# Attention with transposed scores: row scores issued two units ahead, in two PSUM banks instead of three, transposed scores two blocks ahead in three

## The reference

```python
def sink_attention(qg, k, v, sink, valid):       # 8 heads of 64, 2 key heads
    s = jnp.einsum('bqhgd,bkhd->bhgqk', qg, k).astype(jnp.float32) * ATTN_SCALE
    if valid is not None:
        s = jnp.where(valid, s, NEG_INF)         # window of +-128 tokens, and 256 context tokens
    ...
    p = jax.nn.softmax(jnp.concatenate([s, sink_col], axis=-1), axis=-1)[..., :-1]
    return jnp.einsum('bhgqk,bkhd->bqhgd', p, v.astype(jnp.float32))
```

## Time and profile before

| what | us |
|---|---|
| median of 3 runs (lowest, highest) | 3675.62 (3671.17, 3679.07) |
| profiled execution, device time | 3673.01 |
| its span, first to last instruction | 3671.2 |
| TensorE busy in the span | 2980.1 (81%) |
| VectorE busy | 1621.3 (44%) |
| ScalarE busy | 1228.6 (33%) |
| mean granted TensorE clock | 0.896 |

### The profile page before, as it was taken

How to read it: one execution, slowest core, us unless ns; L and a number is a source line. 1 busy time by engine, 2 the same in 40 slices (tenths; PEclk the granted TensorE clock), 3 DMA queues, 4 the chain that set the end, 5 groups by cost and what they waited for, 6 DMA issues and landing times. The chain is left out here.

```text
span 3671.2 us, 36461 instructions
## 1 busy us (share of the span) xinstructions
PE 2980.1 (81%) x14078; PEld 2311.5 (63%) x14078; DVE 1621.3 (44%) x2617; ACT 1228.6 (33%) x1972; POOL 160.5 (4%) x258
## 2 busy tenths in 40 slices
PE   7799997857775979996894799999788288848893
PEld 2577874536664848884663689888555166737773
DVE  1566334537774130005552335421233453347786
ACT  2444212434553041113422321111233211227786
POOL 0000000100000000000000000000000010020002
PEclk9899998988997979996887999999899588869997
DMA  5233333236202013211204023332231642259996
GB/s 217 86 123 130 132 108 80 61 87 169 65 22 99 13 62 124 91 69 64 89 24 167 17 80 117 113 99 86 85 80 47 248 133 69 94 192 378 362 385 257
DMA packets 144305, 452.02 MB, mean 123 GB/s; under 512 B 18259, under 2 KB 39379, under 8 KB 142837
## 3 DMA queue, kind: packets, MB, share of 16 engines
q1 hardware_dynamic: 100196, 280.78, 22.7%
q0 software_dynamic: 27520, 98.02, 7.6%
q10 hardware_dynamic: 16416, 70.90, 5.3%
HBM read 322.68 MB, written 126.95 MB: 122 GB/s over the span
## 5 line engine op out<-in xcount | busy, mean ns | idle before, releaser
L948 PE MATMUL acc<-act_hi,w_hi 128*128 128x512 f32 (+3 forms) x2512 | 706.0, 379 | 202.2 <-PEq L967 109.6
L948 PE MATMUL acc<-act_lo,w_hi 128*128 128x512 f32 (+3 forms) x2512 | 686.4, 371 | 0.0
L948 PE MATMUL acc<-act_hi,w_lo 128*128 128x512 f32 (+3 forms) x2512 | 684.5, 370 | 0.0
L948 PEld LDWEIGHTS acc<-act_hi,w_hi 128*128 128x128 f32 x2512 | 450.9, 192 | 298.4 <-issue 218.5
L730 DVE TENSOR_TENSOR w_lo<-w_stage,w_hi 128x1024 fp32r<-128x1024 f32 x114 | 139.7, 1225 | 919.9 <-ACT w_hi L616 919.9
L948 PEld LDWEIGHTS acc<-act_lo,w_hi 128*128 128x128 f32 x2512 | 447.7, 191 | 80.7
L948 PEld LDWEIGHTS acc<-act_hi,w_lo 128*128 128x128 f32 x2512 | 446.5, 190 | 79.0
L616 ACT ACTIVATE w_hi<-w_stage 128x1024 fp32r<-128x1024 f32 x114 | 120.8, 1060 | 1073.8 <-PE acc L948 1073.8
L2661 DVE TENSOR_TENSOR expert_lo<-expert_stage,expert_hi 128x1024 fp32r<-128x1024 f32 x186 | 226.0, 1224 | 77.2 <-ACT expert_hi L2604 74.9
L2604 ACT ACTIVATE expert_hi<-expert_stage 128x1024 fp32r<-128x1024 f32 x186 | 195.7, 1058 | 88.6 <-DMA expert_stage<-in_exp_w 46.5
L1717 DVE TENSOR_REDUCE max<-scores 128x1 f32<-128x256 f32 (+6 forms) x256 | 114.4, 482 | 191.4 <-PE scores L1840 190.5
(11 more groups left out here) (360 smaller groups left out, 4272.3 us busy)
## 6 DMA issues: line engine op xcount, KB each, us to landing
expert_stage<-in_exp_w SPq DMA_DIRECT2D x186, 512.0 KB, 6.5
w_stage<-in_w_in SPq DMA_DIRECT2D x43, 512.0 KB, 4.3
rope<-out_stage ACTq DMA_DIRECT2D x26, 640.0 KB, 3.6
proj<-out_stage ACTq DMA_DIRECT2D x26, 640.0 KB, 5.2
slots_in<-zero SPq DMA_DIRECT2D x1, 15872.0 KB, 42.3
residual<-slots_in POOLq DMA_DIRECT2D x31, 512.0 KB, 7.1
slots_out<-residual POOLq DMA_DIRECT2D x31, 512.0 KB, 6.7
w_stage<-in_ab_w_in SPq DMA_DIRECT2D x26, 512.0 KB, 5.0
```

What stands on the lines that cost most here:

```text
L948: mmi = eng.matmul(a[:, t, 0:n], lhs[:, j.w % 2, kb:kb + P], rhs[:, c0 + k, off:off + n], start=first, stop=last)
```

## The change

Row scores are issued two units ahead instead of one, spread over all the blocks of a unit, in two banks instead of three. Transposed scores have three banks and are issued two blocks ahead of the value product. The transposes of the next unit's maxima stand in the first block's slot, behind the values' transposes, and ScalarE's copy stands behind its second exponential. The queries get a fourth buffer, the keys of the decay attention a third; the gate's loads stand apart from the queries'; and the values are loaded first.

```diff
-        VS, CS, R = min(NV, 2), min(NCK, 2), 4 if sink else 2
+        VS, CS, R, QS = min(NV, 2), min(NCK, 3), 4 if sink else 2, 4
...
-        SP = [ps(f"scores{i}", [P, 512]) for i in range(3)]
-        ST = [ps(f"scores_t{i}", [P, 512]) for i in range(2)]
+        SP = [ps(f"scores{i}", [P, 512]) for i in range(2)]
+        ST = [ps(f"scores_t{i}", [P, 512]) for i in range(3)]
...
         def pieces_at(n, b):
-            B, M = len(units[n].blocks), len(units[n + 1].pieces) if n + 1 < NU else 0
-            slots = max(B - 1, 1)
-            return range(M * b // slots, M * (b + 1) // slots) if b < slots else range(0)
+            B, M = len(units[n].blocks), len(units[n + 2].pieces) if n + 2 < NU else 0
+            return range(M * b // B, M * (b + 1) // B)
...
+            load_values(0)
             load_keys(0)
             load_queries(0)
-            load_values(0)
+            if NU > 1:
+                load_queries(1)
...
-                at.setdefault(max(0, last_of_chunk[c - 1] - len(units) // NCK + 1), []).append((load_keys, c))
+                at.setdefault(last_of_chunk[c - CS] + 1 if c >= CS else 0, []).append((load_keys, c))
...
-                if n + 1 < NU:
-                    load_queries(n + 1)
+                if n + 2 < NU:
+                    load_queries(n + 2)
+                if sink:
+                    load_gate(n)
...
                     exps(n, b)
                     if b == 0 and n >= 1:
                         root(n - 1)
-                    if b == max(B - 2, 0) and sink and n + 1 < NU:
-                        sinks(n + 1)
-                if n + 1 < NU:
-                    copy_rows(n + 1)
+                    if b == min(1, B - 1) and n + 1 < NU:
+                        copy_rows(n + 1)
+                if sink and n + 2 < NU:
+                    sinks(n + 2)
...
                 for i in range(min(2, M)):
-                    reduce(n + 1, i)
+                    reduce(n + 2, i)
                 if n >= 1:
                     output(n - 1)
+                if sink and QS <= n + 3 < NU:
+                    eng.wait_ge(st_done, blocks_before[n])
+                    eng.memset(q2[64:66, (n + 3) % QS, :].bitcast(F32), 0.0).then_inc(cleared, 1)
                 for i in range(2, M):
-                    reduce(n + 1, i)
-                if n + 1 < NU:
-                    combine(n + 1)
+                    reduce(n + 2, i)
+                if n + 2 < NU:
+                    combine(n + 2)
...
-                if p >= 3:
-                    eng.wait_ge(max_done, p - 2)
+                if p >= 2:
+                    eng.wait_ge(max_done, p - 1)
...
-                if q >= 2:
-                    eng.wait_ge(exped, q - 1)
+                if q >= 3:
+                    eng.wait_ge(exped, q - 2)
...
+                if B > 1:
+                    scores_t(n, 1)
                 for b in range(B):
-                    if b + 1 < B:
-                        scores_t(n, b + 1)
+                    if b + 2 < B:
+                        scores_t(n, b + 2)
                     if b == 0:
                         for vg in values_at[n]:
                             values_t(*vg)
+                        if n + 1 < NU:
+                            rows_t(n + 1)
                     for i in pieces_at(n, b):
-                        pre(n + 1, i)
-                    if b == B - 1 and n + 1 < NU:
-                        rows_t(n + 1)
+                        pre(n + 2, i)
                     pv(n, b)
```

More of the change, by code:

```diff
@@ L1537, in wide_attention_phase @@
         NTP = NB * P
-        VS, CS, R = min(NV, 2), min(NCK, 2), 4 if sink else 2
+        VS, CS, R, QS = min(NV, 2), min(NCK, 3), 4 if sink else 2, 4
         NPC = max(pc for u in units for _, pc, _, _, _ in u.pieces) + 1
-        qs, q2 = (sb(n, [P, 3, 512], F32R) for n in ("q_stack", "q_rows"))
+        qs, q2 = (sb(n, [P, QS, 512], F32R) for n in ("q_stack", "q_rows"))
         kh, kl = (sb(n, [P, CS, NTP], F32R) for n in ("k_hi", "k_lo"))
@@ L1556, in wide_attention_phase @@
              "v_loaded", "set_up", "select_loaded", "select_ready", "max_rows_cleared", "dve_steps"))
-        q_in = [sem(f"q_loaded{i}") for i in range(3)]
-        k_in = [sem(f"k_loaded{i}") for i in range(2)]
+        q_in = [sem(f"q_loaded{i}") for i in range(QS)]
+        k_in = [sem(f"k_loaded{i}") for i in range(CS)]
         gate_in = [sem(f"gate_loaded{i}") for i in range(3)]
@@ L1621, in load_queries @@
             def load_queries(n):
-                u, s = units[n], n % 3
-                if n >= 3:
-                    eng.wait_ge(st_done, blocks_before[n - 2])
+                u, s = units[n], n % QS
+                if n >= QS:
+                    eng.wait_ge(st_done, blocks_before[n - QS + 1])
                 for i in range(NP):
@@ L1628, in load_queries @@
                     eng.dma_start(part(q2[0:64, s, :].bitcast(F32), i), u.qh[i]).then_inc(q_in[s], 16)
[L1629 to L1634, removed]
+                if fox:
                     if n == 0:
@@ L1637, in load_queries, with load_gate @@
                     eng.dma_start(q2[64:70, s, :].bitcast(F32), u.frow).then_inc(q_in[s], 16)
+            def load_gate(n):
+                if n >= 3:
+                    eng.wait_ge(out_ready, n - 2)
+                for i in range(NP):
+                    eng.dma_start(part(gate[:, n % 3, :], i), units[n].gate[i]).then_inc(gate_in[n % 3], 16)
+            load_values(0)
             load_keys(0)
             load_queries(0)
-            load_values(0)
+            if NU > 1:
+                load_queries(1)
             if sink:
@@ L1689, in copy_rows @@
                 eng.wait_ge(t_done, t_no["rows", n] + 1)
-                eng.activation(q2[64:64 + R, n % 3, :], TR[0:R, :], ACT.Copy).then_inc(t_copied, 1)
-            if sink:
-                sinks(0)
+                eng.activation(q2[64:64 + R, n % QS, :], TR[0:R, :], ACT.Copy).then_inc(t_copied, 1)
+            for n in range(min(2, NU)):
+                if sink:
+                    sinks(n)
             copy_rows(0)
@@ L1787, in _ @@
                 eng.tensor_copy(sel[:], sel_raw[:]).then_inc(sel_ready, 1)
-            for i in range(len(units[0].pieces)):
-                reduce(0, i)
-            combine(0)
+            for n in range(min(2, NU)):
+                for i in range(len(units[n].pieces)):
+                    reduce(n, i)
+                combine(n)
             for n in range(NU):
-                M = len(units[n + 1].pieces) if n + 1 < NU else 0
+                M = len(units[n + 2].pieces) if n + 2 < NU else 0
                 for vg in values_at[n]:
@@ L1886, in _ @@
                 pre(0, i)
+            if NU > 1:
+                for i in range(len(units[1].pieces)):
+                    pre(1, i)
             rows_t(0)
```

31 lines of the change are left out of this document (14 added, 17 removed).

## The result

The changed kernel takes 3616.77 us (median of 4 runs, 3605.74 to 3617.93) against 3674.24 us (median of 4 runs, 3671.17 to 3679.07): 0.9836 of the time, 95% interval 0.9813 to 0.9858. Forecast were 3611 us and a range of 3598 to 3645.

What follows compares the result with a forecast made beforehand. TensorE's queue was taken as the bound, its idle and slow time as what can be gained; gains of 79.8 us less 14.8 made 65.0 off 3673.0, and 2.6 added for the median gave 3611, range 3598 to 3645.

Steps and rivals of the forecast that it cites:

- waits for `rows`, sink: Sink attention: TensorE's waits before the maxima's transposes go, gaining 26.7 us, and one wait for a maximum, 1.3.
- two banks, units 8 to 10: Sink units 8 and 9, with four row scores in a slot, wait at the two score banks: 3.5 us lost.
- waits for `rows` and `q_rows`, decay: Decay attention: waits before the maxima's transposes and for ScalarE's copy go, gaining 26.9 us, less 1.5 for thin cover.
- clock, decay: Decay attention: the granted clock no longer falls at seven passages from nine-block to five-block units, gaining 11 us.
- values' wait, decay: Decay attention: the maxima's transposes wait for VectorE's copy of the next pair's values in the same bank, 7.8 us lost.
- the narrow cover: Decay attention: a five-block unit's three transposed scores make 1.3 us against about 1.4 needed, 1.5 us lost in all.
- in a five-block sink unit there are one or two row scores in a slot of about 2 us, so nothing waits: Ordinary sink units: two score banks instead of three cost no wait, since VectorE reduces each in 0.42 to 0.56 us.
- waits for a maximum in ordinary units: Sign named beforehand that the prediction is wrong; it expected 4 to 6 us of them only around the context units.
- The second rival: Two banks make TensorE wait in ordinary units, the output standing ahead of a reduction; 3636 to 3641 us, chance 0.14.
- the step on the start: Sink attention's start: values loaded first, the first row score then waits for the last query transfer, at 564.8; gain 7.0 us.
- the row scores of unit 1 at the start: Now ahead of the first transposes, they fill a 1.75 us wait but wait for the first combination; 0.5 us lost.
- The rival that the clock falls within units: Short waits at the two banks lower the clock once in each of 36 units, costing 61 us: 3685, chance 0.03.

Runs made afterwards that it cites:

- e9: Changed kernel with two banks for transposed scores, issued one block ahead, one bank unused; sink 228.9, decay 211.7, whole 3612.28 us.
- e2: Changed kernel with three banks for row scores and two for transposed ones, issued one block ahead; sink 218.8, decay 205.2, whole 3602.67 us.
- e5: Kernel before, with values loaded ahead of keys and queries at each phase's start; sink 247.6, decay 237.5, whole 3663.24 us.
- e1: Changed kernel with the select matrix loaded directly behind the first values; sink 227.3, decay 210.8, whole 3617.02 us.
- e7: Changed kernel with the edits of e1, e2 and e3 together; 3584.62 us, 0.9756 of before; sink 215.6, decay 200.6.
- e4: Kernel before, with useless matmuls in the pauses at the decay attention's passages from nine to five blocks; decay 234.2, whole 3666.27 us.
- e3: Changed kernel with the next pair's values transposed two blocks later, VectorE's copy behind its first two reductions; sink 230.6, decay 204.0, whole 3612.72 us.
- e6: Changed kernel with the maxima's transposes back at the unit's end and ScalarE's copy behind the last exponential; sink 231.7, decay 209.4, whole 3619.06 us.

## Why the prediction was right, and where it was not

The forecast of 3611 missed by 6 us. That it came so near is partly luck: the sink attention was forecast 8.7 too good and the decay attention 2.9 too bad. The terms, in the order of its working:

| term | forecast | shown |
|---|---|---|
| waits for `rows`, sink | 26.7 + 1.3 | gone; ordinary unit 12.15 to 10.83 once the order is mended (e9, e2) |
| clock, sink | 2.2 | both falls gone (1.00 from 32 to 223 us behind the memset); not priced by itself |
| two blocks ahead, sink | 0 | -3.8 |
| two banks, units 8 to 10 | -3.5 | -3.1 (e2), 2.2 of it the row banks (e9) |
| start, sink | +7.0 - 0.5 | first row score 7.9 earlier, 6.8 by itself (e5); then -3.6 (e1) and -4.8 (e1 to e7) |
| waits for `rows` and `q_rows`, decay | 26.9 - 1.5 | 28.0 |
| clock, decay | 11 | 11.1 (e4) |
| values' wait, decay | -7.8 | -6.7 (e3) |
| start, decay | 4.7 | first row score 4.7 earlier, 4.7 by itself (e5) |
| ends of the phases | -1.0 - 0.5 | not measured by themselves |

The 28.0 is worked out from units: four units take 51.43 in e4, which has the waits but not the clock's loss, and 43.96 in e3, which has neither; 7.47 less in four is 28.0 in fifteen.

**Right.** The reading of the bound (TensorE's queue, idle by what VectorE and ScalarE still owe), the two mechanisms of the lost time (the pause, and the clock behind it), and the place and size of the new values' wait. Experiments with one cause each bear out all three. The decay attention came out 2.9 better by small errors on one side: the narrow cover that I charged with 1.5 costs nothing, the waits were worth 1.1 more than counted, the values' wait 1.1 less; that is 3.7, and the 0.8 against it I have not assigned.

**Wrong: the sink attention, 8.7 too good.** Three steps failed. First, the step "in a five-block sink unit there are one or two row scores in a slot of about 2 us, so nothing waits" counted slots as equal. They are not: two blocks ahead, the last two slots of a unit have no transposed score, and a row score meets VectorE behind its output, 0.37 us in each of ten units. The prediction named waits for a maximum in ordinary units as a sign that it is wrong, and there they are (0.93 on the weight load). The second rival named this place, the output ahead of a reduction, with a price of 0.7 a unit and more; it has half the price, and it takes TensorE's order to bring it about. Second, the step on the start followed the last query transfer, and not what else stood behind twelve of them in SP's queue: the select matrix, 3.6. Third, it priced the row scores of unit 1 at the start by their place alone (0.5), and never asked what two banks do at a low clock: 4.8. Those are 12.2 us. The terms that are left would make the sink attention 3.0 slower than e7 shows it, and 0.9 of that is the first row score; the rest I have not assigned. The rival that the clock falls within units is wrong for steady units (1.00 over 60 us). But short waits at the two banks went with a clock that stayed low at the start, where it had not been looked for.

**Open.** Why the clock falls behind pauses of 0.73 and 0.40 us at the passages and not behind those of 1.12 in sink units or of 0.35 to 0.40 in e6 is not settled; e4 shows only that filling the pauses keeps it up. Nor does the length of the pauses alone decide it: behind the pauses of 1.17 and 0.55 at the passages from five to nine blocks it stayed up in the kernel before, and fell once each in e4 and e5. The time at which it rises in the decay attention varies between executions without a cause that I found. And no run takes apart the added query and key buffers or the gate's own loads; the changed kernel's waits for query loads are 1.3 us at the sink attention's start and 0.2 in the decay attention.

## What to carry to other kernels

When an order is shifted by a unit, count for every slot what is left in it and who must answer within it: the average slot says nothing, and a pause may be booked on the weight load and not on the matmul. A spare PSUM bank belongs where the slower answer is, here VectorE's reductions and not ScalarE's exponentials: that exchange, with the order that goes with it, was worth 15 us. And where loads are moved forward in a queue, look for the small one that is now last.

## What the hardware did that I had not expected

At the start of a phase, the time in which the clock stays at 0.50 depended on how many banks lay between two engines that take turns: with two (e1), TensorE ran 4 us stretches with 3.5 us of work at 0.50; with three (e7), the clock rose 10 us earlier. And five matmuls that compute nothing, placed in the pauses of 0.73 and 0.40 us at a passage, gave back 1.58 us each time, more than the pauses themselves.
